# A three-block transformer kernel on one core: low parts of a turn's last tile placed behind the output's first tile, convolution taps placed elsewhere, and tiles begun in pairs

## The reference

```
def reference(...):
    x = first_block(...)    # stick-breaking attention (16 heads), SwiGLU with D_FF = 2816, gated side input p
    x = second_block(...)   # modulated norm; a causal convolution of 31 taps, gated and normed, then a
                            # pointwise product; retention with 4 heads (256 wide); one output product
    x = third_block(...)    # S5 (64 groups, complex states) with a GLU, SSD (16 heads), output product, p_3
    return x

def rms_norm(x, g):         # before every large product
    return x * lax.rsqrt(mean(x * x) + 1e-6) * g

# second block, cut
a = conv_a * sigmoid(conv_bp)
a = causal_depthwise_conv(a, conv_w, conv_b)          # 31 taps
a = silu(layernorm(a, conv_ln_g, conv_ln_b)) @ conv_pw
y_conv = a * silu(conv_gate)
q, k = rotary(q), rotary(k) * 256 ** -0.5
y_ret = groupnorm(retention(q, k, v)) * silu(ret_gate)
h = h + gate * (concat([y_conv, y_ret]) @ w_out)
```

## Time and profile before

| | |
|---|---|
| runs, median (lowest to highest) | 4154.89 us (4148.94 to 4157.69), 3 runs |
| the profiled execution, its own time | 4153.42 us |
| its span | 4151.6 us |
| TensorE matmul busy | 3840.0 us (92%) |
| VectorE busy | 2210.1 us (53%) |
| ScalarE busy | 902.8 us (22%) |
| GpSimd busy | 1041.6 us (25%) |
| chain that ended last | TensorE 82%, VectorE 12%, ScalarE 2% |
| mean granted TensorE clock | 0.943 |

### The profile page before, as it was taken

One profiled execution on the slowest core, in us unless ns is written; L12 is line 12 of the kernel. 1 busy time (PEld: TensorE's weight loads), 2 busy tenths in 40 slices (PEclk: granted clock), 3 DMA queues, 4 the chain that ended last, 5 costly groups with the idle time before them and its releaser, 6 DMA issues.

```text
span 4151.6 us, 47406 instructions
## 1 busy us (share of the span) xinstructions
PE 3840.0 (92%) x19082; PEld 3102.2 (75%) x19082; DVE 2210.1 (53%) x2823; ACT 902.8 (22%) x1635; POOL 1041.6 (25%) x581
## 2 busy tenths in 40 slices
PE   6999998999999999999989998798999978889998
PEld 5677676788888887888866776577788767778777
DVE  5554557332323266999334523646254994653565
ACT  3434335200000032111010011302111012542131
POOL 1111111344444432333211211131322311003322
PEclk9999999999999999999999998898999986779999
DMA  2000000211212111222211212121553234222111
GB/s 88 21 26 23 29 26 16 71 66 56 66 56 66 63 43 36 87 86 81 71 51 36 71 42 76 44 64 46 138 117 79 81 87 122 62 60 81 61 51 61
DMA packets 139241, 260.25 MB, mean 63 GB/s; under 512 B 45632, under 2 KB 87616, under 8 KB 136000
## 3 DMA queue, kind: packets, MB, share of 16 engines
q1 hardware_dynamic: 72208, 156.26, 13.3%
q10 hardware_dynamic: 66864, 101.63, 7.2%
HBM read 209.35 MB, written 46.14 MB: 62 GB/s over the span
## 4 chain that ended last, share of the span: by engine, by line
PE 82%; DVE 12%; ACT 2%; issue 2%; DMA 1%; SPq 1%; POOL 1%; ACTq 0%; DVEq 0%; POOLq 0%
PE bank L572 22%; PE bank L574 22%; PE bank L573 22%; PE bank L784 2%; PE bank L954 2%; PE bank L821 1%; PE bank L691 1%; PE bank L804 1%; PE bank L943 1%; PE bank L1082 1%; DVE fb L1962 1%; DVE hn L1817 1%; DVE h L2315 1%; DVE xl L1828 1%; DVE ab L1965 1%
## 5 line engine op out<-in xcount | busy, mean ns | idle before, releaser
L572 PE MATMUL bank<-xh,wh 128*128 128x512 f32 x3008 | 1198.0, 398 | 75.1 <-DVE xl L1828 19.2
L573 PE MATMUL bank<-xl,wh 128*128 128x512 f32 x3008 | 1182.2, 393 | 0.0
L574 PE MATMUL bank<-xh,wl 128*128 128x512 f32 x3008 | 1180.9, 393 | 0.0
L529 POOL CAST wh<-raw 128x1024 fp32r<-128x1024 f32 x264 | 282.4, 1070 | 3004.9 <-PE bank L574 2951.3
L572 PEld LDWEIGHTS bank<-xh,wh 128*128 128x128 f32 x3008 | 571.4, 190 | 235.3 <-issue 38.3
L531 POOL TENSOR_TENSOR wl<-raw,wh 128x1024 fp32r<-128x1024 f32 x264 | 673.6, 2552 | 21.1
L574 PEld LDWEIGHTS bank<-xh,wl 128*128 128x128 f32 x3008 | 571.3, 190 | 121.4
L573 PEld LDWEIGHTS bank<-xl,wh 128*128 128x128 f32 x3008 | 572.3, 190 | 114.5
L2109 DVE SCALAR_TENSOR_TENSOR bank<-apad,cols,bank 128x512 f32<-128x512 f32 x406 | 267.9, 747 | 0.0
L1864 DVE TENSOR_TENSOR h<-bank,h 128x512 f32<-128x512 f32 x240 | 165.3, 690 | 153.3 <-PE bank L574 152.4
L1962 DVE TENSOR_TENSOR_SCAN fb<-fb 128x256 f32<-128x256 f32 (+7 forms) x128 | 189.5, 1521 | 73.6 <-ACT ab L1262 73.6
(11 more groups left out here) (340 smaller groups left out, 5408.1 us busy)
## 6 DMA issues: line engine op xcount, KB each, us to landing
raw<-in_wstream SPq DMA_DIRECT2D x264, 512.0 KB, 3.6
spills<-spill ACTq DMA_DIRECT2D x40, 512.0 KB, 2.7
rawm<-in_mod_w ACTq DMA_DIRECT2D x12, 1024.0 KB, 4.9
gate_spill<-gates ACTq DMA_DIRECT2D x16, 512.0 KB, 2.6
tabs<-in_rope ACTq DMA_DIRECT2D x4, 2048.0 KB, 8.5
f<-spills SPq DMA_DIRECT2D x8, 1024.0 KB, 5.7
h<-in_x ACTq DMA_DIRECT2D x4, 1024.0 KB, 11.8
tabs<-gate_spill ACTq DMA_DIRECT2D x4, 1024.0 KB, 7.0
```

The source lines that it names most:

```text
L529: nc.gpsimd.tensor_copy(wh[:, slot], raw[:, slot]).then_inc(S("panel_high"), 1)
L572: nc.tensor.matmul(o, lh, rh, start=start, stop=False)
L573: nc.tensor.matmul(o, lh, rl, start=False, stop=False)
L574: return nc.tensor.matmul(o, ll, rh, start=False, stop=stop)
```

## The change

1. In five stages the first two tiles are made as a pair (`first_pair`): for half 0, then for half 1, TensorE takes each slab for the first tile as its low part arrives, and for the second tile two slabs later (`PAIR_LAG`). Units then go half by half (`pair_unit`), so the first eviction of each tile stands among the norm's steps, behind step 9 or 11 (`PAIR_TAKEN`; in `pw` the high parts behind 10 and 12). The split of the third and fourth panel waits for the third and fourth unit (`FIRST_FREED`), where it waited for the second and the fourth. Buffers that are written that early move in memory (`fb` is put first, `yt` last), and the first load of `cg` is issued before the high parts.
2. The taps: behind the second tile of K none any more, and in the steps six at step 4 (`TAPS_STEP`) in place of one each at steps 0, 3, 6 and 9.
3. In `pw` and `glu` the low parts of the last tile of "in" i + 1 stand behind the adds of the first tile of "out" i.

The diff, cut to its core:

```
+PAIR_LAG = 2
+FIRST_FREED = [3, 4]
+def pair_unit(m, th, paired=True):
+    return 2 * th + m if paired else 2 * m + th
+PAIR_TAKEN = [9, 11]
+def pair_tile(u, paired=True):
+    return (u % 2, u // 2) if paired else (u // 2, u % 2)
...
     start = [key for name in ("q0", "k0", "v0") for key in project(name)]
+    start[:4] = [start[n] for n in (0, 2, 1, 3)]
+    unit_of.update({key: n for n, key in enumerate(start)})
+    freed[:2] = FIRST_FREED
...
+            def freed_after(name, i, m):
+                if i is None and m < 2 and name in ("ffn_first", "conv", "pw", "s5_u"):
+                    return FIRST_FREED[m]
+                return PANEL_UNITS[name][m]
...
+            def first_pair(unit, panel, norm):
+                split_done(panel + 1)
+                slots = [(panel.b + m) % 2 for m in range(2)]
+                for th in range(2):
+                    t = slice(th * HALF, (th + 1) * HALF)
+                    for step in range(KT + PAIR_LAG):
+                        if step < KT:
+                            pe.wait_ge(S("norm_low"), SPLIT0[norm] + th * KT + step + 1)
+                        for m in range(2):
+                            k = step - PAIR_LAG * m
+                            if not 0 <= k < KT:
+                                continue
+                            if k == 0:
+                                bank_free(unit + pair_unit(m, th))
+                            mm = mm3(banks[m][:, :], wh[:, slots[m], k, :], wl[:, slots[m], k, :], xh[:, k, t],
+                                     xl[:, k, t], k == 0, k == KT - 1)
+                            if k == KT - 1:
+                                mm.then_inc(S("unit_done"), 1)
...
-            for key in ATTN_START:
+            first_pair(units("attn"), panels("attn"), "mix")
+            for key in ATTN_START[4:]:
                 attn_project(key)
...
-            norm_highs("mix")
+            norm_highs("mix", taken={PAIR_TAKEN[0]: lambda: attn_take(("q", 0, 0))})
...
+                norm_highs("ffn", taken={PAIR_TAKEN[0]: lambda: hidden_gate(units("ffn_first"), 0)})
...
+                norm_highs("first_final", "mod", {PAIR_TAKEN[j]: lambda j=j: conv_take(0, j, 0) for j in range(2)})
...
+                gates_load(0)
+                norm_highs("conv_ln", "silu", {PAIR_TAKEN[u] + 1: lambda u=u: pw_high(0, u) for u in range(2)})
...
+                norm_highs("second_final", taken={
+                    PAIR_TAKEN[m]: lambda m=m: spill_tile(units("s5_u"), m, 0, m, ACT.Copy, True) for m in range(2)})
...
                 for i in range(2 * KT):
                     scale(i)
                     if i:
                         low(i - 1)
+                    if i in taken:
+                        taken[i]()
                 low(2 * KT - 1)
...
+            norm_split("mix", gain("norm_mix"), taken={PAIR_TAKEN[1]: lambda: attn_take(("k", 0, 0))})
...
+                norm_split("ffn", gain("norm_ffn"), taken={
+                    PAIR_TAKEN[1]: lambda: hidden_product(units("ffn_first"), units("ffn_first") + 1, 0)})
...
+                norm_split("conv_ln", gain("conv_ln_g_2"), "silu", cv,
+                           {PAIR_TAKEN[u]: lambda u=u: pw_gate(0, u) for u in range(2)})
...
-                    last_taps(2)
+                    if x == 0:
+                        last_taps(2)
                 for s, c0 in enumerate(ret_col):
-                    if s % 3 == 0:
-                        last_taps(1)
+                    if s == TAPS_STEP:
+                        last_taps(6)
...
+                def pw_last_low(i):
+                    for u in (2, 3):
+                        pw_low(i, u)
                 for kind, i in TURN_ORDER:
                     if kind == "out":
-                        add_tiles(unit, lambda n: mod[:, 16 + n:17 + n], norm="second_final" if i == 3 else None)
+                        add_tiles(turn_unit("pw", "out", i), lambda n: mod[:, 16 + n:17 + n],
+                                  norm="second_final" if i == 3 else None,
+                                  then=lambda n: pw_last_low(i + 1) if n == 0 and i < 3 else None)
                         continue
...
                     if kind == "out":
                         add_tiles(unit, half_way=(lambda: side_low(2)) if i == 3 else None,
-                                  norm="ple3" if i == 3 else None)
+                                  norm="ple3" if i == 3 else None,
+                                  then=lambda n: glu_low(i + 1, 1) if n == 0 and i < 3 else None)
                         continue
...
+                        if m == 0 or i == 0:
+                            glu_low(i, m)
```

More of the change, by code:

```diff
@@ L548, in turn @@
                 for m in range(PANELS[name]):
-                    split(panels(name, i) + m, before[m] if m < 2 else units(name, i) + PANEL_UNITS[name][m - 2])
+                    split(panels(name, i) + m, before[m] if m < 2 else units(name, i) + freed_after(name, i, m - 2))
                     if m in MOD_AFTER.get(name, {}):
@@ L560, in _ @@
                     for i in range(1, n):
-                        turn(name, i, [units(name, i) + (PANEL_UNITS[name][dp - 2 + m] - UNITS[name])
+                        last = None if i == 1 else i - 1
+                        turn(name, i, [units(name, i) + (freed_after(name, last, dp - 2 + m) - UNITS[name])
                                        for m in range(2)])
@@ L851, in hidden @@
                 def hidden(unit, panel, split=None):
-                    for m in range(4):
-                        tile_x(unit + 2 * m, panel + m, split=split if m == 0 else None)
+                    if split is not None:
+                        first_pair(unit, panel, split)
+                    for m in range(2 if split is not None else 0, 4):
+                        tile_x(unit + 2 * m, panel + m)
                 hidden(units("ffn_first"), panels("ffn_first"), "ffn")
@@ L883, in side_product, with plain @@
                          [(ph[:, t, :], pl[:, t, :]) for t in range(2)])
-            def plain(name, split=None):
+            def plain(name, split=None, paired=False):
                 for i in turns(pe, TURNS[name]):
+                    if paired and isinstance(i, int):
+                        first_pair(units(name), panels(name), split)
+                        continue
                     for m in range(2):
@@ L904, in _ @@
                 for i in turns(pe, KT):
-                    for m in range(4):
-                        tile_x(units("conv", i) + 2 * m, panels("conv", i) + m,
-                               split="first_final" if isinstance(i, int) and m == 0 else None)
+                    if isinstance(i, int):
+                        first_pair(units("conv"), panels("conv"), "first_final")
+                    for m in range(2 if isinstance(i, int) else 0, 4):
+                        tile_x(units("conv", i) + 2 * m, panels("conv", i) + m)
                 pe.wait_ge(S("h_kept"), 2 * KT)
@@ L1000, in hidden_and_out @@
                     if kind == "in":
+                        if split is not None and i == 0:
+                            first_pair(unit, panel, split)
+                            continue
                         for m in range(2):
-                            tile_x(unit + 2 * m, panel + m, in_high, in_low,
-                                   split=split if i == 0 and m == 0 else None)
+                            tile_x(unit + 2 * m, panel + m, in_high, in_low)
                     else:
@@ L1377, in _ @@
                 gate_take("gate1", 0, "first_final")
-            if "conv" in run:
-                norm_highs("first_final", "mod")
             def conv_store(n):
@@ L1509, in _, with spill_tile, spill_tiles @@
                 norm_root("second_final")
[L1511 removed]
+            def spill_tile(unit, m, th, u, func, permuted):
+                produced(act, unit + u)
+                bank = (unit + u).b % 2
+                o, b = spill[:, m, th * HALF:(th + 1) * HALF], banks[bank][:, :]
+                if permuted:
+                    q = S5_BLOCKS // 2
+                    o = spill[:, m, :].rearrange("p (t b) -> p b t", t=S5_TAU)[:, th * q:(th + 1) * q, :]
+                    b = b.rearrange("p (b t) -> p b t", t=S5_TAU)
+                A(o, b, func).then_inc(S(f"bank_free{bank}"), 1)
+            def spill_tiles(name, first, func, permuted=False, paired=False):
                 for i in turns(act, 4):
@@ L1515, in spill_tiles @@
                     unit = units(name, None if isinstance(i, int) else i)
+                    together = paired and isinstance(i, int)
+                    if together:
+                        for u in range(2, 4):
+                            spill_tile(unit, u % 2, u // 2, u, func, permuted)
                     for m in range(2):
@@ L2085, in conv_input @@
                 for th in range(2):
-                    evicted(dve, unit + th)
-                    evicted(dve, unit + (2 + th))
```

(8 more changed lines are left out.)

224 lines of the change are left out of this document (116 added, 108 removed).

## The result

The changed kernel takes 4097.5 us (median of 4 runs, 4093.2 to 4106.1) against 4152.7 beside it: 0.9867 of the time, 95% interval 0.9849 to 0.9885, so 55 us less. The prediction said 44 us less, 4111 (range 4100 to 4127). The direction was right; the gain is 8 to 11 us larger than the sum. The profiled execution is the slowest of the first four (4106.1 us), so profile against profile only 47.3 us are gained. That difference has to be explained too.

What follows compares the result with a forecast made beforehand. The chain of waits is mostly TensorE, so gains must shorten its waits. Eight terms, from 11.6 (pw's start) to −2.9 (FFN's start), sum to 43.8 us; against the 4154.9 median that gives 4111, range 4100 to 4127.

Steps and rivals of the forecast that it cites:

- the FFN loses: Start of FFN: chain of load, modulation split and panel split stays, TensorE restarts after 10 us idle; loss 2.9 us.
- I take no lower clock for it: Behind each pair: TensorE's 1.8 us idle is not followed by lower clock; if it were, 1.4 us each.
- Taps in the heads: Retention heads: 7.8 us of waits go, 1.5 to 1.8 come back as clock dips; gain 6.0 us.
- Turns of pw: Three in-to-out changes in pw: 2.6 idle + 1.4 clock − 0.7 late adds, 3.3 us each, 10.0 in all.
- Turns of glu: Three in-to-out changes in glu: only the low parts' 1.46 us leave the path; 1.4 each, 4.2 us.
- Start of s5_u: Start of stage s5_u: third tile at 2900.8 where the second tile ended at 2904.8; gain 4.0 us.
- what comes behind each place follows TensorE: Everywhere outside the changed places: later work moves along with TensorE, no further gain or loss.
- The second: Rival: glu's dips go (4.2), heads keep their full 7.8 (1.8), splits behind pairs overlap better; 4103 us, chance 0.15.
- The first: Rival: idle behind pairs lowers the clock (conv, pw, s5_u: 4.2), FFN's 2.9 loss doubles; 4118 us, chance 0.15.
- the third: Rival: POOL holds up moved low parts ahead of second tile's adds; both turn stages' 14.2 us stay away; 4125, chance 0.13.
- The fourth: Rival: evictions slow the norm so much that pairs end when the two tiles did; 4128 us, chance 0.05.
- the fifth: Rival: TensorE is granted less clock or stays low long after the FFN start's idle; 4163 or more, chance 0.02.

Runs made afterwards that it cites:

- e6: Changed kernel with the FFN's first modulation weights loaded before the high parts and split behind the third panel: 4091.4 us, 0.985 of the kernel before.
- e1: Kernel before with only the taps of the heads placed as in the change: 4142.8 us, 0.9976 of the kernel before.
- e4: Changed kernel run once more with no edit, for a second profile: 4101.2 us.
- e9: Kernel before with only the load of pw's gate tiles issued before the norm's high parts: 4145.5 us, 0.9985 of the kernel before.
- e2: Kernel before with only the turns' low parts in pw and glu moved behind the output's first tile: 4134.7 us, 0.9961 of the kernel before.
- e7: Changed kernel with glu's last product of a turn also moved behind the output's first tile: 4088.7 us, 0.9844 of the kernel before.
- e12: Changed kernel with pw's two low parts one VectorE instruction earlier, between the first output tile's two adds: 4103.6 us, 0.9888 of the kernel before.
- e8: Changed kernel with the edits of e6 and e7 together: 4080.9 us, 0.9825 of the kernel before.
- e10: e8 with PAIR_LAG 4 in place of 2: 4075.4 us, 0.9819 of the kernel before.
- e3: Changed kernel with taps and the turns' low parts put back, leaving pairs and early gate load: 4126.8 us, 0.9935 of the kernel before.
- e5: Changed kernel with the FFN's start as before, two tiles one after the other: 4097.8 us, 0.9871 of the kernel before.

## Why the prediction was right and wrong

**Right.** The mechanism of every part. The pair is bound by TensorE (in s5_u matmuls run without a gap from 2840.05 to 2862.1, 22.0 us against 22.1), the split behind it leaves 1.63 to 1.72 us idle (1.8), the FFN loses (2.0 to 4.4 against 2.9, and e6 shows its chain; from 735 us on, behind the stretches of clock ahead of it, it is 2.9 to 3.4 in all four pairings of the profiles), conv gains 6.0 (5.9), pw's start 9.0 to 11.5 (11.6), of which the load 6.3 (6). "I take no lower clock for it" held behind each 1.6 to 1.7 us of idle. Attention gained 3.6 to 4.6, not 5.0: its V units start at 61.38 (61.1 was forecast), 4.8 us ahead of the earlier trace rows, and in the first pair 1.1 us of that is lost to the lower clock right behind.

**Wrong.** Four terms were too small, by 12.4 us together, and some 9.5 of these are lower clock that went, where the prediction took it to stay or to come back.
- *Taps in the heads*, "1.5 to 1.8 come back", gain 6.0. It is the step that failed most. The waits gave 8.6 (7.8), and the clock gave more instead of taking: e1 has 9.6 by the medians, the profiles 10.2 to 13.8. The control was misread: head 3 took 1.5 us longer than head 0 behind its first values, and the prediction took that for the price of a short wait. The first sums of heads 1 and 2, before, and of heads 0 to 2, after, show that it is not:

```profile
2268.24 0.70 PE L968 MATMUL bank<-ot,mats 128*128 128x512 f32 x1 [1.18 <-ACT ot L1439]
...
2415.34 0.70 PE L968 MATMUL bank<-ot,mats 128*128 128x512 f32 x1 [1.18 <-ACT ot L1439]
```

```profile
2114.62 0.70 PE L1021 MATMUL bank<-ot,mats 128*128 128x512 f32 x1 [1.18 <-ACT ot L1503]
...
2259.39 0.70 PE L1021 MATMUL bank<-ot,mats 128*128 128x512 f32 x1 [1.18 <-ACT ot L1503]
...
2402.80 0.70 PE L1021 MATMUL bank<-ot,mats 128*128 128x512 f32 x1 [1.18 <-ACT ot L1503]
```

  Before, head 1 had the same long wait as head 0 (6.55 us ahead of its first values, at 2235.57) and took 2268.24 − 2235.57 = 32.7 us, as long as head 3; head 2 had 3.90 us, at 2382.99, and took 32.4. After, with waits of 2.8 us, heads 0, 1 and 2 take 31.3, 31.2 and 31.2 (31.3, 32.7 and 31.2 in e4). The 1.5 us lie in one head or another whatever the wait. The granted clock of heads 0, 1 and 2, each from its first matmul to the next head's, before and after, shows no such price (window, TensorE busy with its matmuls, granted clock, DMA share, GB/s):

```profile
2080.16:2227.37 147.21, 135.20 (x633) 0.94 0.16 50
2227.37:2377.44 150.07, 138.06 (x633) 0.92 0.15 50
2377.44:2524.37 146.93, 137.56 (x633) 0.93 0.16 51
```

```profile
2078.99:2223.91 144.92, 136.65 (x633) 0.94 0.16 51
2223.91:2367.37 143.46, 135.20 (x633) 0.95 0.16 52
2367.37:2510.75 143.38, 135.12 (x633) 0.95 0.16 52
```

  The three heads give 2.3, 6.6 and 3.6 us, where the idle alone would give 3.75, 3.76 and 1.11: the clock is the same in one and higher in two. One control head, with one stretch of lower clock, was no measure.
- *Turns of pw*, "the next adds end 0.7 us too late", gain 3.3 each. It is 4.0 each, 2.6 of idle + 1.4 of clock: the 0.7 didn't happen. It assumed 2708.4 for the end of the low parts, which is their old end beside POOL; behind the first tile's adds they start as POOL ends, take 1.35 us, and the next add is done before TensorE needs its bank.
- *Turns of glu*, 1.4 each. It is 2.0 each: the idle gave 1.4 (3.79 to 2.40), and behind the shorter one 7, 7 and 6 matmuls are at 0.43 us where 12, 6 and 10 were.
- *Start of s5_u*, 4.0. From its first matmul to its third tile it gave 4.0. Another 3.3 us lie ahead of it, where TensorE ends pw and the norm; that stretch before and after:

```profile
2860.19:2876.97 16.78, 14.95 (x84) 0.59 0.10 32
```

```profile
2826.48:2840.05 13.57, 11.73 (x82) 0.75 0.13 39
```

  The matmuls are all but the same ones (84 and 82 by the edges of the windows), and nothing there was edited. e9 and e2, which don't touch s5_u, have 3.1 and 2.3 us of the same, and e6, e7 and e12, which keep its pair, have nothing of it. So the 3.3 us are no gain of the pair; where the lower clock falls changes with edits far ahead.

By the mean of the two pairs of profiles these four exceed their terms by 5.3 + 2.1 + 1.8 + 3.2 = 12.4 us (only the heads' 0.8 and pw's 2.1 are idle time); attention, FFN and pw's start miss theirs by 0.9 + 0.3 + 1.4. That is the 10 us between 43.8 and the 53.8 that the places gave on average. One more term was put at nothing, "what comes behind each place follows TensorE": everywhere else the profiles lose 4.6 and 8.4 us. Profile against profile the two errors nearly cancel (47 us against 44), which is luck and no merit of the sum.

**The rivals.** The second (dips in glu go, the heads keep their 7.8, splits overlap better) had the right sign and 4103, and holds in part: the heads gave more than 7.8, glu's dips only got shorter (1.8 of its 4.2 us), and the idle behind the pairs is 1.63 to 1.72 us where the sum had 1.8. The first fell (no lower clock behind 1.6 to 1.7 us of idle), and so did the third, by the rows of pw's turn above, although e12 shows how near it was. The fourth and the fifth did not come: the pair in s5_u lasts 22 us, and the clock granted over the whole span is 0.943 in both profiles.

**What stays open.** What puts a stretch of lower clock where it is, in places that have the same instructions and the same gaps. The 1.6 us directly behind glu are there in both profiles of the changed kernel and in e2, e6, e7, e8, e9, e10 and e12, and not in e1, e3 and e5; the 1.9 at the end are there in the same ones (1.7 to 2.6) but for e7. Nor do these runs show why the lower clock inside the heads became less along with the waits (by 11.3 − 8.6 = 2.7 us on average, by 5.2 in e1). Executions of one kernel lie up to 22 us apart (e2: 4125.3 to 4147.4); in e1 the fastest, 4134.4, was granted 0.947 and the slowest, 4149.0, 0.943.

## What to carry to other kernels

Price an idle gap of TensorE that goes together with the lower clock behind it, as a term of its own, and as a range: behind gaps of 3.8 us in glu there were 0 to 13 matmuls at 0.43 us, up to 2.6 us. Don't let it "come back" without a row that shows where, and hold a control against every case at hand: head 1 would have shown that head 3's 1.5 us had nothing to do with its wait. When instructions are moved to another place of an engine's queue, take their duration from the new place: with GpSimd at work next to VectorE, one instruction earlier or later decided between 1.35 and 2.72 us, and between no wait and one. Where a shortened stage only uncovers the next wait (the FFN), follow the chain behind it at once: taking one load and one split out of it was worth 9.5 us, a fifth of the whole change.

## What the runs showed of the hardware

The fourteen profiles have 196 idle gaps of TensorE of 0.9 us and more that lie between unbroken matmuls of 512 columns at full granted clock. Behind those of 1.06 to 1.74 us (37, behind pairs and in turns) no matmul came at 0.43 us. Behind those of 2.38 to 2.45 us in the turns of pw and glu (33) 6 to 8 came, every time; in many cases TensorE first made one to three matmuls 0.23 us apart, and those at 0.43 followed.

In between, the length of the gap doesn't decide. The wait of 1.80 us for `gl` (matmul starts 1477.95 before and 1476.54 after) was followed by full clock in eight profiles, the one of before among them, and by 7 or 8 matmuls at 0.43 us in six, the one of the changed kernel among them. The wait of 2.31 us for `y5l` ahead of glu was followed by full clock in thirteen of fourteen (the granted clock is 1.00 in the 6 us from 3761.6 in the changed kernel, and 0.72 in those from 3747.6 in e5). A gap of 2.39 us in e12, ahead of the matmul at 2996.77, had no matmul at 0.43 us behind it either. And in e9, behind the three gaps of 3.77 us in glu's turns, there were 12, 5 and none; the first and the last:

```profile
3841.81 0.80 PE L572 MATMUL bank<-xh,wh 128*128 128x512 f32 x1 [3.77 <-DVE h L1868]
...
3941.74 0.50 PE L572 MATMUL bank<-xh,wh 128*128 128x512 f32 x1 [3.77 <-DVE h L1868]
```

A longer gap didn't mean a longer stretch either: behind 9.69 us there were 9 such matmuls, behind 3.79 us 12.
